# Attention part of a decoder layer: queries scaled once, negated maxima, one reciprocal per head, the normalising multiplications on GpSimd, and one value product in five in full f32 instead of two

## Chip, cores and metric

One core of one Trainium2 chip runs the whole program. The time is the device time of one execution in microseconds (us); of several runs the median counts. Granted TensorE clock 1.00 in a profile is the level of 2.4 GHz, 0.50 that of 1.2 GHz.

## What is computed

One decoder layer over 1024 tokens of width 1024: an input projection, retention heads, sparse-attention heads, an output projection, a gated MLP with a short convolution, an embedding gate and a last norm. The change touches only the sparse-attention heads (8 query heads, 2 key/value groups, head width 64). Cut to what matters, for a block of queries:

```python
s = einsum(qi, ck) * scale                       # compressed keys: 63
p_c = masked_softmax(s, ...);  o_c = einsum(p_c, cv)
s = einsum(qi, ksel) * scale                     # selected keys: with 16 blocks of 64, all of them
p_s = masked_softmax(s, ...);  o_s = einsum(p_s, vsel)
s = einsum(qi, kwi) * scale                      # window of 512 keys
p_w = masked_softmax(s, ...);  o_w = einsum(p_w, vwi)
o = gates[0] * o_c + gates[1] * o_s + gates[2] * o_w

def masked_softmax(s, mask):
    s = where(mask, s, -inf)
    m = max(s);  m = where(isfinite(m), m, 0)
    e = exp(s - m)
    return e / maximum(sum(e), 1e-30)
```

## The kernel before

The kernel is written engine by engine, with semaphores by hand, and each engine runs its instructions in the order written. A product of two f32 values is made of f32r products of a high part and a low part: ScalarE (ACT) copies a tile to its high part, VectorE (DVE) subtracts to get the low part (helper `low`, L1813).

The attention part takes 16 **rounds**, v = 0 to 15: round v is the token tile t = v // 2 (128 queries) and the group v % 2, with four heads. A head has two branches. Branch 0 is the selected keys, (t+1)·128 columns of scores in PSUM banks 0 and 1; branch 1 is the window (up to 640 columns) and the 63 compressed keys, in banks 2 and 3. Heads times branches give 8 **slots** a round, numbered n. For slot n:

- TensorE (PE) makes the scores (`qk`, L1334 to L1347). It may do so when the exponentials of slot n-2, which read the same banks, are done.
- DVE takes the maxima (L1861; L1863 and L1864) and makes the bias of the exponentials `nb` (L1869).
- ACT makes the exponentials (L932; L936 and L939) into `prob` in SBUF, with their sums in `den`.
- DVE, one slot later, guards the sums (L1874), inverts them (L1879) and multiplies `prob` by the inverse and the gate (L1889; L1893 and L1896).

The probabilities of round v are used during round v+1, from its second slot on: PE transposes them 128 keys at a time (`turn_p`, L1261, four heads at once, into one of three PSUM banks), ACT copies the bank (`p_high`, L949), and PE multiplies the values by it (`output`). A list written by `plan_attention` sets the order: turn j, then output j-2, spread over the 8 slots; round v has 3, 5, 7, 9, 11, 12, 13 or 14 tiles of keys for t = 0 to 7. A tile is **whole** or **split**. A whole tile is copied once to `ptw` and multiplied in full f32 (L1377, one instruction that the trace shows as two records). A split tile is copied to its high part `pth`, DVE makes the low part `ptl` (`p_low`, L1813), and PE makes two f32r products (L1379, L1380). `pth` with `ptl` has two places, `ptw` has two more; the copy of a tile waits until the output that used its place before is done (`freed_by`). Within a slot the order is, on PE: turns and outputs, then the scores of the next slot; on ACT: copies, then the exponentials; on DVE: maxima, guard, bias, inverse, low parts, then the multiplications.

```python
def whole(st):
    return st[0] == "turn_p" and st[2] % 5 in (0, 2)
```

Of the kernel before, what the change touches and what calls it, by code (L numbers as in the profile page):

```python
# [15 lines left out]
P = 128  # L16
S = 1024
# [6 lines left out]
G = 2  # L24
RG = QH // G
# [3 lines left out]
WIN_T = 4  # L29
# [79 lines left out]
def build(nc, xt, x, pt, pos, cst_d, wmix_d, wffn_d, gnw, w_in, cpos, ck_w1, ck_w2, cv_w1, cv_w2,  # L109
# [8 lines left out]
    with ctx:  # L118
        def sem(name):
            return ctx.enter_context(nc.semaphore(name))  # L120
# [102 lines left out]
        comb = a.put("comb", [P, 2, 2 * P], F32)  # L223
        mx = a.put("mx", [P, 4, 2], F32)
        nb = a.put("nb", [P, 4, 2], F32)
        den = a.put("den", [P, 4, 2], F32)
        rd = a.put("rd", [P, 4, 2], F32)
        rd2 = a.put("rd2", [P, 4, 2], F32)
        assert a.at <= 229344, a.at


# [158 lines left out]
        def ret_slots(s, k, table):  # L390
# [17 lines left out]
        tr_full, tr_h, tr_l = sem("tr_full"), sem("tr_h"), sem("tr_l")  # L408
        qk_done, nb_done, exp_done, norm_done, pv_done = (
            sem("qk_done"), sem("nb_done"), sem("exp_done"), sem("norm_done"), sem("pv_done"))  # L410
        swap_done, csum_done, nsah_done, nsal_done = sem("swap_done"), sem("csum_done"), sem("nsah_done"), sem("nsal_done")

        h_in, wfb_in = sem("h_in"), sem("wfb_in")
# [57 lines left out]
        def whole(st):  # L471

            return st[0] == "turn_p" and st[2] % 5 in (0, 2)

        outs_of = {(v, j): n for n, (v, j) in enumerate(st[1:] for st in plan if st[0] == "output")}

# [207 lines left out]
        def _(pool):  # L686
# [45 lines left out]
            for s in range(NS + 1):  # L732
                for k in range(NK):
# [3 lines left out]
                        ret_load(0)  # L737
                    ret_slots(s, k, table)

            for t in range(NT):  # L740
# [9 lines left out]
        def _(act):  # L750
# [158 lines left out]
            def q_split_high(st):  # L909
                v = st[1]  # L910
                act.wait_ge(aqr_in[v % 2], 16 * (v // 2 + 1))
                if v:
                    act.wait_ge(tr_full, turns_of["turn_q", v - 1] + 1)
                nc.scalar.activation(aq2[:, :, 0], aqr[:, v % 2].rearrange("p (r d) -> p r d", r=RG), ACT.Copy).then_inc(aqh_done, 1)

            def q_turned(st):
                v = st[1]
# [5 lines left out]
            def exponentials(v, i):  # L923
                n, t = 2 * RG * v + i, v // G
                r_, br = divmod(i, 2)
                act.wait_ge(nb_done, n + 1)
                if v >= 2:
                    act.wait_ge(tr_full, turns_of["turn_p", v - 2, len(key_tiles(v - 2)) - 1] + 1)
                s_, pr = ps[:, 2 * br:2 * br + 2, :].rearrange("p a n -> p (a n)"), prob[:, v % 2, r_]
                m = n % 4  # L930
                if br == 0:
                    nc.scalar.activation(pr[:, 0:(t + 1) * P], s_[:, 0:(t + 1) * P], ACT.Exp, bias=nb[:, m, 0:1],  # L932
                                         scale=SCALE, accum_out=den[:, m, 0:1]).then_inc(exp_done, 1)
                else:
                    w = (t - max(0, t - WIN_T) + 1) * P
                    nc.scalar.activation(pr[:, S:S + w], s_[:, 0:w], ACT.Exp, bias=nb[:, m, 0:1], scale=SCALE,  # L936
                                         accum_out=den[:, m, 0:1])
                    at = S + (WIN_T + 1) * P
                    nc.scalar.activation(pr[:, at:at + NCMP], s_[:, 5 * P:5 * P + NCMP], ACT.Exp, bias=nb[:, m, 1:2],  # L939
                                         scale=SCALE, accum_out=den[:, m, 1:2]).then_inc(exp_done, 1)  # L940

            def p_high(st):
                at = place_of[st]
# [167 lines left out]
        def _(pe):  # L1111
# [237 lines left out]

            def p_turn(st):  # L1350
                v, j = st[1:]
                _, _, at, w = key_tiles(v)[j]
                pe.wait_ge(norm_done, 2 * RG * (v + 1))
                turn_free(st)
                for r_ in range(RG):
                    mm = transpose_f(ps[0:w, turn_bank(st), r_ * P:(r_ + 1) * P], prob[:, v % 2, r_, at:at + w])
                mm.then_inc(tr_full, 1)
# [217 lines left out]
        def _(dve):  # L1575
# [274 lines left out]
            def q_split_low(st):  # L1850
                v = st[1]
                dve.wait_ge(aqh_done, v + 1)
                low(aq2[:, :, 1], aqr[:, v % 2].rearrange("p (r d) -> p r d", r=RG), aq2[:, :, 0]).then_inc(aql_done, 1)

            def row_max(v, i):
                n, t, br = 2 * RG * v + i, v // G, i % 2
                dve.wait_ge(qk_done, n + 1)
                m = n % 4
                s_ = ps[:, 2 * br:2 * br + 2, :].rearrange("p a n -> p (a n)")
                if br == 0:  # L1860
                    return mark(nc.vector.reduce_max(mx[:, m, 0:1], s_[:, 0:(t + 1) * P], AX_X))  # L1861
                w = (t - max(0, t - WIN_T) + 1) * P
                nc.vector.reduce_max(mx[:, m, 0:1], s_[:, 0:w], AX_X)  # L1863
                return mark(nc.vector.reduce_max(mx[:, m, 1:2], s_[:, 5 * P:5 * P + NCMP], AX_X))  # L1864

            def exp_bias(v, i, maxima):
                m, w = (2 * RG * v + i) % 4, 1 + i % 2
                dve.wait_ge(dve_chain, maxima)
                nc.vector.tensor_scalar(nb[:, m, 0:w], mx[:, m, 0:w], FLOOR, -SCALE, ALU.max, ALU.mult).then_inc(nb_done, 1)  # L1869

            def guard_sum(v, i):
                n, w = 2 * RG * v + i, 1 + i % 2
                dve.wait_ge(exp_done, n + 1)
                return mark(nc.vector.tensor_scalar(rd[:, n % 4, 0:w], den[:, n % 4, 0:w], 1e-30, None, ALU.max))  # L1874

            def invert_sum(v, i, guarded):
                m, w = (2 * RG * v + i) % 4, 1 + i % 2
                dve.wait_ge(dve_chain, guarded)
                return mark(nc.vector.reciprocal(rd2[:, m, 0:w], rd[:, m, 0:w]))  # L1879

            def normalize(v, i, inverted):

                n, (t, g_), (r_, br) = 2 * RG * v + i, divmod(v, G), divmod(i, 2)
                m, hd = n % 4, g_ * RG + r_
                dve.wait_ge(dve_chain, inverted)
                pr = prob[:, v % 2, r_]
                if br == 0:
                    p_ = pr[:, 0:(t + 1) * P]
                    nc.vector.tensor_scalar(p_, p_, rd2[:, m, 0:1], gates[:, t, hd, 1:2], ALU.mult, ALU.mult).then_inc(norm_done, 1)  # L1889
                else:  # L1890
                    width = (t - max(0, t - WIN_T) + 1) * P
                    p_ = pr[:, S:S + width]
                    nc.vector.tensor_scalar(p_, p_, rd2[:, m, 0:1], gates[:, t, hd, 2:3], ALU.mult, ALU.mult)  # L1893
                    at = S + (WIN_T + 1) * P
                    p_ = pr[:, at:at + NCMP]
                    nc.vector.tensor_scalar(p_, p_, rd2[:, m, 1:2], gates[:, t, hd, 0:1], ALU.mult, ALU.mult).then_inc(norm_done, 1)  # L1896

            def p_low(st):
                at = place_of[st]
# [32 lines left out]
            q_split_low(("split_q", 0))  # L1932
            for n, slot in enumerate(slots):
                lows = [st for st in slot if st[0] in ("turn_p", "turn_ret") and not whole(st)]
                if n < 2 * RG * NV:
                    maxima = row_max(*divmod(n, 2 * RG))
                if 0 < n <= 2 * RG * NV:
                    guarded = guard_sum(*divmod(n - 1, 2 * RG))
                if n < 2 * RG * NV:
                    exp_bias(*divmod(n, 2 * RG), maxima)  # L1940
                if 0 < n <= 2 * RG * NV:
                    inverted = invert_sum(*divmod(n - 1, 2 * RG), guarded)
                for st in lows:
                    {"turn_p": p_low, "turn_ret": ret_low}[st[0]](st)
                if 0 < n <= 2 * RG * NV:
                    normalize(*divmod(n - 1, 2 * RG), inverted)
# [183 lines left out]
```

## Time and profile before

| | |
|---|---|
| median of 3 runs | 1711.2 us (1708.43 to 1711.42) |
| profiled execution, its time | 1707.47 us |
| its span | 1705.7 us |
| PE busy over the span | 1638.8 us (96%) |
| DVE busy | 1038.6 us (61%) |
| ACT busy | 628.3 us (37%) |
| GpSimd (POOL) busy | 78.1 us (5%) |

The shares are means over parts that differ. The attention rounds lie at about 432 to 747 us of the span. PE's busy time holds the overlap of pipelined matmuls and can hold waits of a few tenths of a microsecond, so the distance from one PE start to the next says more than it.

### The profile page before, as it was taken

The page shows a single profiled execution, that of the slowest core. Times are in us where ns is not written, and L with a number is a line of the kernel's source. Part 1 is how long each engine was busy: PE and PEld are TensorE (multiplying, and loading weights), DVE is VectorE, ACT ScalarE, POOL GpSimd, SP SyncE. Part 2 cuts the span into 40 slices and gives each one's busy share as a digit, 9 for nine tenths or more (in the row PEclk, how much of TensorE's full clock was granted, in tenths as well). Part 3 has the DMA queues.
Part 4 walks back from the last instruction along what each step waited for, and adds up shares of the span by engine and source line. Part 5 has one row for each costly group of instructions (what it writes and reads, how often), then busy time and mean ns, then how long its engine had stood idle before and what let it go on. Part 6 is the DMA issues. An engine that isn't in the chain of part 4 may idle for free.

```text
span 1705.7 us, 22210 instructions
## 1 busy us (share of the span) xinstructions
PE 1638.8 (96%) x8157; PEld 1326.4 (78%) x8157; DVE 1038.6 (61%) x2063; ACT 628.3 (37%) x1173; POOL 78.1 (5%) x126
## 2 busy tenths in 40 slices
PE   8899999998789999999999999999999999999997
PEld 6688888888556776678888888888888888888885
DVE  6833556655799999964345555555556565556432
ACT  6214443344677777752222211221221122114221
POOL 0111221121000000000000000000000000000000
PEclk9899999998799999999999999999999999999998
DMA  5433233225000000060121211111121111122000
GB/s 197 130 99 117 93 109 103 82 92 190 25 23 17 13 13 1 1 235 1 40 72 38 74 37 37 58 52 37 37 74 37 37 46 65 37 72 102 25 38 37
DMA packets 48989, 110.62 MB, mean 65 GB/s; under 512 B 8848, under 2 KB 17040, under 8 KB 48912
## 3 DMA queue, kind: packets, MB, share of 16 engines
q1 hardware_dynamic: 41488, 85.47, 15.0%
q0 software_dynamic: 7424, 24.12, 4.2%
q8 instruction: 48, 0.79, 0.2%
q14 instruction: 29, 0.24, 0.0%
HBM read 89.65 MB, written 19.92 MB: 64 GB/s over the span
## 4 chain that ended last, share of the span: by engine, by line
PE 85%; DVE 6%; ACT 2%; issue 2%; DVEq 0%; POOLq 0%; POOL 0%; ACTq 0%
PE ps L1461 27%; PE ps L1115 14%; PE ps L1117 14%; PE ps L1116 14%; PE ps L1261 4%; PE ps L1377 3%; PE ps L1334 2%; PE ps L1340 1%; PE ps L1448 1%; PE ps L1284 1%; PE ps L1379 1%; PE ps L1120 1%; PE ps L1380 1%; DVE mx L1863 1%; DVE ptl L1813 1%
## 5 line engine op out<-in xcount | busy, mean ns | idle before, releaser
L2003 DVE TENSOR_TENSOR h<-h,ps 128x512 f32<-128x512 f32 x336 | 225.4, 686 | 148.7 <-PE ps L1117 147.5
L1461 PE MATMUL ps<-htl,wuh 128*128 128x512 f32 x672 | 209.7, 393 | 0.0
L1461 PE MATMUL ps<-hth,wuh 128*128 128x512 f32 x672 | 209.6, 393 | 0.0
L1461 PE MATMUL ps<-hth,wul 128*128 128x512 f32 x672 | 209.6, 393 | 0.0
L1115 PE MATMUL ps<-wh,xth 128*128 128x512 f32 (+1 forms) x448 | 186.7, 417 | 14.8 <-DVE wl L1595 13.2
L1117 PE MATMUL ps<-wh,xtl 128*128 128x512 f32 (+1 forms) x448 | 170.8, 381 | 0.0
L1116 PE MATMUL ps<-wl,xth 128*128 128x512 f32 (+1 forms) x448 | 170.3, 380 | 0.0
L1059 ACT ACTIVATE ffh<-ffa 128x1024 fp32r<-128x1024 f32 x22 | 23.3, 1060 | 369.8 <-DVE ffa L2030 369.8
L1461 PEld LDWEIGHTS ps<-hth,wuh 128*128 128x128 f32 x672 | 126.3, 188 | 29.3
L1461 PEld LDWEIGHTS ps<-hth,wul 128*128 128x128 f32 x672 | 126.2, 188 | 29.1
L1461 PEld LDWEIGHTS ps<-htl,wuh 128*128 128x128 f32 x672 | 126.3, 188 | 28.8
L1116 PE MATMUL ps<-wdl,ffh 128*128 128x512 f32 x352 | 139.5, 396 | 0.0
L1117 PE MATMUL ps<-wdh,ffl 128*128 128x512 f32 x352 | 139.1, 395 | 0.0
L1115 PE MATMUL ps<-wdh,ffh 128*128 128x512 f32 x352 | 139.1, 395 | 0.0
L2020 DVE SCALAR_TENSOR_TENSOR act__166<-gate,taps,act__166 128x1024 f32<-128x1024 f32 x22 | 28.3, 1285 | 128.6 <-ACT act__166 L1052 128.6
L1115 PEld LDWEIGHTS ps<-wh,xth 128*128 128x128 f32 x448 | 86.2, 192 | 23.9 <-DVE xtl L1603 7.5
L1261 PE MATMUL ps<-cst,prob 128*128 128x128 f32 (+1 forms) x592 | 88.7, 278 | 9.7 <-DVE retl L1813 7.8
L1117 PEld LDWEIGHTS ps<-wh,xtl 128*128 128x128 f32 x448 | 85.3, 190 | 16.3
L1334 PE MATMUL ps<-aks,aqt 128*128 128x512 f32 (+3 forms) x192 | 80.7, 420 | 16.1 <-ACT prob L939 14.5
L1261 PEld LDWEIGHTS ps<-cst,prob 128*128 128x128 f32 (+1 forms) x592 | 69.4, 142 | 33.8 <-issue 24.5
L1116 PEld LDWEIGHTS ps<-wl,xth 128*128 128x128 f32 x448 | 86.3, 193 | 8.7
L1115 PEld LDWEIGHTS ps<-wdh,ffh 128*128 128x128 f32 x352 | 66.2, 188 | 15.8
(270 smaller groups left out, 3180.2 us busy)
## 6 DMA issues: line engine op xcount, KB each, us to landing
wuraw<-in_w_up SPq DMA_DIRECT2D x44, 512.0 KB, 5.0
wraw<-in_w_in SPq DMA_DIRECT2D x48, 256.0 KB, 3.3
proj_d<-stage POOLq DMA_DIRECT2D x48, 256.0 KB, 2.3
wdraw<-in_w_down SPq DMA_DIRECT2D x22, 512.0 KB, 3.6
rin<-proj_d POOLq DMA_DIRECT2D x32, 256.0 KB, 4.2
xraw<-in_xt SPq DMA_DIRECT2D x16, 256.0 KB, 6.4
owraw<-in_w_out SPq DMA_DIRECT2D x8, 512.0 KB, 5.7
h<-in_x SPq DMA_DIRECT2D x1, 4096.0 KB, 15.9
```

The lines of the kernel that those rows point to most:

```text
L1059: nc.scalar.activation(ffh[:, u], ffa[:], ACT.Copy).then_inc(ffh_done, 1)
L1115: first = nc.tensor.matmul(out, wh_, xh_, start=start, stop=False)
L1116: nc.tensor.matmul(out, wh_, xl_, start=False, stop=False)
L1117: return first, nc.tensor.matmul(out, wl_, xh_, start=False, stop=stop)
L1120: return nc.tensor.transpose(out.bitcast(F32R), in_, ident_r[:])
L1261: return nc.tensor.transpose(out, in_, ident_f[0:n, 0:n])
L1284: mm = nc.tensor.matmul(ps[:, 6 + i, half * G * NCMP:(half + 1) * G * NCMP], cw1[:, i, j, half * P:(half + 1) * P], cb[:, i, j], start=(j ...
L1334: nc.tensor.matmul(ps[:, bank, 0:w], q_, aks[:, br, g_, at:at + w], start=True, stop=False)
L1377: mm = nc.tensor.matmul(out_, vals.bitcast(F32), ptw[0:w, at], start=first, stop=last)
L1461: mm = nc.tensor.matmul(ps[:, 2 * part + half, :], w_, x_[:, k, half * 512:(half + 1) * 512], start=(k == 0 and i == 0), stop=(k == NK - 1 ...
L2003: nc.vector.tensor_tensor(hh, hh, ps[:, 4 + o_ % 4, :], ALU.add).then_inc(dn_add, 1)
L2020: nc.vector.scalar_tensor_tensor(act_[:], gate[:, 1:S + 1], taps[:, u, 1:2], act_[:], ALU.mult, ALU.add).then_inc(conv_mid, 1)
```

## The change

Five edits, all in the attention rounds. The scale goes into the high and low parts of the queries, so the exponentials need none. The maxima come out negated, straight into `nb` for two of the three; the third goes through one small minimum. The sums of a head's three branches are guarded and inverted once, every second slot. The multiplications of `prob` go to GpSimd, which runs three a head, waiting for the inverse; a turn of a branch-0 tile waits for all but the last of them. And a tile is whole only where its number is a multiple of five.

```diff
-        den = a.put("den", [P, 4, 2], F32)
-        rd = a.put("rd", [P, 4, 2], F32)
-        rd2 = a.put("rd2", [P, 4, 2], F32)
+        den = a.put("den", [P, 4, 3], F32)
+        rd = a.put("rd", [P, 4, 3], F32)
...
-            return st[0] == "turn_p" and st[2] % 5 in (0, 2)
+            return st[0] == "turn_p" and st[2] % 5 == 0
...
+            def normalize(v, r_):
+
+                n, (t, g_) = RG * v + r_, divmod(v, G)
+                hd = g_ * RG + r_
+                pool.wait_ge(inv_done, INV0 + n + 1)
+                pr = prob[:, v % 2, r_]
+                p_ = pr[:, 0:(t + 1) * P]
+                nc.gpsimd.tensor_scalar(p_, p_, rd[:, n % 4, 1:2], gates[:, t, hd, 1:2], ALU.mult, ALU.mult).then_inc(norm_done, 1)
+                p_ = pr[:, S:S + (t - max(0, t - WIN_T) + 1) * P]
+                nc.gpsimd.tensor_scalar(p_, p_, rd[:, n % 4, 2:3], gates[:, t, hd, 2:3], ALU.mult, ALU.mult)
+                at = S + (WIN_T + 1) * P
+                p_ = pr[:, at:at + NCMP]
+                nc.gpsimd.tensor_scalar(p_, p_, rd[:, n % 4, 0:1], gates[:, t, hd, 0:1], ALU.mult, ALU.mult).then_inc(norm_done, 1)
...
-                pe.wait_ge(norm_done, 2 * RG * (v + 1))
+                pe.wait_ge(norm_done, 2 * RG * (v + 1) - (br == 0))
...
-                    return mark(nc.vector.reduce_max(mx[:, m, 0:1], s_[:, 0:(t + 1) * P], AX_X))
+                    nc.vector.reduce_max(nb[:, m, 0:1], s_[:, 0:(t + 1) * P], AX_X, negate=True).then_inc(nb_done, 1)
+                    return
                 w = (t - max(0, t - WIN_T) + 1) * P
-                nc.vector.reduce_max(mx[:, m, 0:1], s_[:, 0:w], AX_X)
-                return mark(nc.vector.reduce_max(mx[:, m, 1:2], s_[:, 5 * P:5 * P + NCMP], AX_X))
+                maximum = mark(nc.vector.reduce_max(mx[:, m, 1:2], s_[:, 5 * P:5 * P + NCMP], AX_X, negate=True))
+                nc.vector.reduce_max(nb[:, m, 0:1], s_[:, 0:w], AX_X, negate=True)
+                dve.wait_ge(dve_chain, maximum)
+                nc.vector.tensor_scalar(nb[:, m, 1:2], mx[:, m, 1:2], -FLOOR * SCALE, None, ALU.min).then_inc(nb_done, 1)
...
+                if n >= 4:
+                    dve.wait_ge(norm_done, 2 * (n - 4) + 2)
+                nc.vector.reciprocal(rd[:, n % 4], den[:, n % 4]).then_inc(inv_done, 1)
```

On DVE, two slots of a round of t = 7 stood as follows before: a branch-1 slot and a branch-0 slot of the next head (maxima, guard, bias, inverse, low parts `ptl`, multiplications of `prob`).

```order
L1863 TENSOR_REDUCE mx<-ps 128x1
L1864 TENSOR_REDUCE mx<-ps 128x1
L1874 TENSOR_SCALAR rd<-den 128x1
L1869 TENSOR_SCALAR nb<-mx 128x2
L1879 RECIPROCAL rd_122<-rd 128x1
L1889 TENSOR_SCALAR prob<-prob,rd_122,gates 128x1024
L1861 TENSOR_REDUCE mx<-ps 128x1
```

With the change the same two slots of that round read:

```order
L1885 TENSOR_REDUCE mx<-ps 128x1
L1886 TENSOR_REDUCE nb<-ps 128x1
L1888 TENSOR_SCALAR nb<-mx 128x1
L1882 TENSOR_REDUCE nb<-ps 128x1
L1894 TENSOR_SCALAR den<-den 128x1
L1901 RECIPROCAL rd<-den 128x3
L1832 TENSOR_TENSOR ptl<-ps,pth 128x512 x2
```

The large multiplications are gone from DVE's row, the guard and the inverse stand in every second slot, and there are more low parts.

On PE, a round of t = 7 reads so before, from the output of tile 1 on (L1379, L1380: output of a split tile; L1261: a turn; L1334 to L1342: scores of the next slot; L1377: output of a whole tile, here tile 2; then turn 5 and the output of tile 3).

```order
L1379 MATMUL ps<-pth,av_105 128x512
L1380 MATMUL ps<-ptl,av_105 128x512
L1261 MATMUL ps<-cst,prob 128x128 x4
L1334 MATMUL ps<-aks,aqt 128x512
L1340 MATMUL ps<-akx,aqt 128x512
L1334 MATMUL ps<-aks,aqt 128x512
L1340 MATMUL ps<-akx,aqt 128x512
L1342 MATMUL ps<-masks_b,ident_b 128x128
L1377 MATMUL ps<-ptw,av_105 128x512
L1261 MATMUL ps<-cst,prob 128x128 x4
L1379 MATMUL ps<-pth,av_105 128x512
L1380 MATMUL ps<-ptl,av_105 128x512
```

And so with the change, at the same place.

```order
L1398 MATMUL ps<-pth,av_105 128x512
L1399 MATMUL ps<-ptl,av_105 128x512
L1280 MATMUL ps<-cst,prob 128x128 x4
L1353 MATMUL ps<-aks,aqt 128x512
L1359 MATMUL ps<-akx,aqt 128x512
L1353 MATMUL ps<-aks,aqt 128x512
L1359 MATMUL ps<-akx,aqt 128x512
L1361 MATMUL ps<-masks_b,ident_b 128x128
L1398 MATMUL ps<-pth,av_105 128x512
L1399 MATMUL ps<-ptl,av_105 128x512
L1280 MATMUL ps<-cst,prob 128x128 x4
L1398 MATMUL ps<-pth,av_105 128x512
```

Tile 2 is split now. Tile 4, turned ahead of the scores, is a split tile in both; its place in `pth` was tile 1's before, whose output stands ahead of that turn, and is tile 2's now, whose output stands behind the scores.

## Rows read from the trace of the kernel before

**Rows 1.** The page, busy time by engine: us, share, instructions.

```profile
PE 1638.8 (96%) x8157; PEld 1326.4 (78%) x8157; DVE 1038.6 (61%) x2063; ACT 628.3 (37%) x1173; POOL 78.1 (5%) x126
DVE  6833556655799999964345555555556565556432
```

**Rows 2.** Windows: stretch, its length, busy (instructions) by engine, PE clock, DMA.

```profile
432.67:443.19 10.52, 7.83 (x40) 7.07 (x39) 8.34 (x46) 5.50 (x24) 0.00 (x0) 0.50 0.08 25
443.19:548.39 105.20, 89.75 (x530) 62.74 (x530) 99.62 (x388) 77.89 (x247) 0.00 (x0) 0.96 0.07 20
548.39:703.83 155.44, 150.23 (x918) 109.36 (x917) 146.11 (x413) 118.01 (x287) 0.00 (x0) 1.00 0.03 9
703.83:747.50 43.67, 41.03 (x229) 27.99 (x227) 32.70 (x78) 29.80 (x63) 0.00 (x0) 1.00 0.35 133
```

**Rows 3.** Timeline of DVE: first maxima of rounds 5, 6, 14 and 15.

```profile
497.79 0.55 DVE L1861 TENSOR_REDUCE mx<-ps 128x1 f32<-128x384 f32 x1
513.75 0.68 DVE L1861 TENSOR_REDUCE mx<-ps 128x1 f32<-128x512 f32 x1
679.08 1.22 DVE L1861 TENSOR_REDUCE mx<-ps 128x1 f32<-128x1024 f32 x1
703.83 1.22 DVE L1861 TENSOR_REDUCE mx<-ps 128x1 f32<-128x1024 f32 x1
```

**Rows 4.** Lines by form, 431 to 748 us: busy, mean ns, idle before.

```profile
L1813 DVE TENSOR_TENSOR ptl<-ps,pth 128x512 fp32r<-128x512 f32 x72 | 49.0, 682 | 14.5 <-ACT pth L949 13.8
L949 ACT ACTIVATE pth<-ps 128x512 fp32r<-128x512 f32 x72 | 43.1, 598 | 17.9 <-PE ps L1261 17.2
...
L1893 DVE TENSOR_SCALAR prob<-prob,rd,gates 128x640 f32<-128x640 f32 x32 | 19.5, 608 | 0.4
...
L1869 DVE TENSOR_SCALAR nb<-mx 128x2 f32<-128x2 f32 x64 | 10.8, 169 | 0.0
...
L932 ACT ACTIVATE prob<-ps,nb 128x1024 f32<-128x1024 f32 x8 | 8.9, 1112 | 0.5 <-DVE nb L1869 0.5
...
L1889 DVE TENSOR_SCALAR prob<-prob,rd,gates 128x1024 f32<-128x1024 f32 x8 | 6.4, 806 | 0.1
```

**Rows 5.** Timeline of round 5: one branch-1 slot, from scores to scores.

```profile
502.76 0.43 PE L1334 MATMUL ps<-aks,aqt 128*128 128x384 f32 x1
...
503.47 0.21 PE L1347 MATMUL ps<-masks_b,ident_b 128*128 128x64 bf16 x1
...
504.81 0.55 DVE L1863 TENSOR_REDUCE mx<-ps 128x1 f32<-128x384 f32 x1
...
505.72 0.58 ACT L936 ACTIVATE prob<-ps,nb 128x384 f32<-128x384 f32 x1
...
506.84 0.42 PE L1334 MATMUL ps<-aks,aqt 128*128 128x384 f32 x1
```

**Rows 6.** Timeline of PE, a stretch in which it does not wait.

```profile
727.16 1.02 PE L1377 MATMUL ps<-ptw,av 128*128 128x512 f32 x2
728.02 0.60 PE L1261 MATMUL ps<-cst,prob 128*63 128x128 f32 x4
728.38 0.48 PE L1379 MATMUL ps<-pth,av 128*128 128x512 f32 x1
728.69 0.40 PE L1380 MATMUL ps<-ptl,av 128*128 128x512 f32 x1
728.93 1.02 PE L1377 MATMUL ps<-ptw,av 128*128 128x512 f32 x2
```

**Rows 7.** POOL's arithmetic by line: ns min/median/max, first and last start.

```profile
L722 POOL TENSOR_TENSOR gst<-gst,cst x8: 1663/1665/2032, 176.7 to 393.5; 128x8 f32<-128x8 f32 x8
L742 POOL TENSOR_TENSOR hst<-hst,cst x8: 540/544/571, 777.5 to 842.9; 128x1 f32<-128x1 f32 x8
```

**Rows 8.** Waits, 431 to 748 us: waiter, releaser, total us, times, longest.

```profile
PE ps L1261 <- DVE retl L1813: 7.8, 6, 1.8
...
PEld ps L1261 <- DVE prob L1896: 3.8, 9, 1.6
...
PE ps L1261 <- DVE prob L1896: 1.7, 2, 1.1
```

More of the change, by code:

```diff
@@ L410, in build @@
             sem("qk_done"), sem("nb_done"), sem("exp_done"), sem("norm_done"), sem("pv_done"))
+        inv_done, INV0 = red_done, 2
         swap_done, csum_done, nsah_done, nsal_done = sem("swap_done"), sem("csum_done"), sem("nsah_done"), sem("nsal_done")
@@ L738, in _ @@
                     ret_slots(s, k, table)
+            def normalize(v, r_):
[10 more added lines that the diff above has]
+                nc.gpsimd.tensor_scalar(p_, p_, rd[:, n % 4, 0:1], gates[:, t, hd, 0:1], ALU.mult, ALU.mult).then_inc(norm_done, 1)
+            for v in range(NV):
+                for r_ in range(RG):
+                    normalize(v, r_)
             for t in range(NT):
@@ L913, in q_split_high @@
                     act.wait_ge(tr_full, turns_of["turn_q", v - 1] + 1)
-                nc.scalar.activation(aq2[:, :, 0], aqr[:, v % 2].rearrange("p (r d) -> p r d", r=RG), ACT.Copy).then_inc(aqh_done, 1)
+                nc.scalar.activation(aq2[:, :, 0], aqr[:, v % 2].rearrange("p (r d) -> p r d", r=RG), ACT.Copy,
+                                     scale=SCALE).then_inc(aqh_done, 1)
             def q_turned(st):
@@ L929, in exponentials @@
                 s_, pr = ps[:, 2 * br:2 * br + 2, :].rearrange("p a n -> p (a n)"), prob[:, v % 2, r_]
-                m = n % 4
+                m, q = n % 4, n // 2 % 4
                 if br == 0:
                     nc.scalar.activation(pr[:, 0:(t + 1) * P], s_[:, 0:(t + 1) * P], ACT.Exp, bias=nb[:, m, 0:1],
-                                         scale=SCALE, accum_out=den[:, m, 0:1]).then_inc(exp_done, 1)
+                                         accum_out=den[:, q, 1:2]).then_inc(exp_done, 1)
                 else:
                     w = (t - max(0, t - WIN_T) + 1) * P
-                    nc.scalar.activation(pr[:, S:S + w], s_[:, 0:w], ACT.Exp, bias=nb[:, m, 0:1], scale=SCALE,
-                                         accum_out=den[:, m, 0:1])
+                    nc.scalar.activation(pr[:, S:S + w], s_[:, 0:w], ACT.Exp, bias=nb[:, m, 0:1],
+                                         accum_out=den[:, q, 2:3])
                     at = S + (WIN_T + 1) * P
                     nc.scalar.activation(pr[:, at:at + NCMP], s_[:, 5 * P:5 * P + NCMP], ACT.Exp, bias=nb[:, m, 1:2],
-                                         scale=SCALE, accum_out=den[:, m, 1:2]).then_inc(exp_done, 1)
+                                         accum_out=den[:, q, 0:1]).then_inc(exp_done, 1)
             def p_high(st):
@@ L1351, in p_turn @@
                 v, j = st[1:]
-                _, _, at, w = key_tiles(v)[j]
-                pe.wait_ge(norm_done, 2 * RG * (v + 1))
+                br, _, at, w = key_tiles(v)[j]
+                pe.wait_ge(norm_done, 2 * RG * (v + 1) - (br == 0))
                 turn_free(st)
@@ L1852, in q_split_low @@
                 dve.wait_ge(aqh_done, v + 1)
-                low(aq2[:, :, 1], aqr[:, v % 2].rearrange("p (r d) -> p r d", r=RG), aq2[:, :, 0]).then_inc(aql_done, 1)
+                nc.vector.scalar_tensor_tensor(aq2[:, :, 1], aqr[:, v % 2].rearrange("p (r d) -> p r d", r=RG), SCALE,
+                                               aq2[:, :, 0].bitcast(F32), ALU.mult, ALU.subtract).then_inc(aql_done, 1)
             def row_max(v, i):
@@ L1860, in row_max @@
                 if br == 0:
-                    return mark(nc.vector.reduce_max(mx[:, m, 0:1], s_[:, 0:(t + 1) * P], AX_X))
+                    nc.vector.reduce_max(nb[:, m, 0:1], s_[:, 0:(t + 1) * P], AX_X, negate=True).then_inc(nb_done, 1)
+                    return
                 w = (t - max(0, t - WIN_T) + 1) * P
-                nc.vector.reduce_max(mx[:, m, 0:1], s_[:, 0:w], AX_X)
-                return mark(nc.vector.reduce_max(mx[:, m, 1:2], s_[:, 5 * P:5 * P + NCMP], AX_X))
[L1866 to L1877, printed above, removed]
-                dve.wait_ge(dve_chain, guarded)
[L1879 to L1896, printed above, removed]
@@ new lines, in row_max, with guard_sum @@
+                maximum = mark(nc.vector.reduce_max(mx[:, m, 1:2], s_[:, 5 * P:5 * P + NCMP], AX_X, negate=True))
+                nc.vector.reduce_max(nb[:, m, 0:1], s_[:, 0:w], AX_X, negate=True)
+                dve.wait_ge(dve_chain, maximum)
+                nc.vector.tensor_scalar(nb[:, m, 1:2], mx[:, m, 1:2], -FLOOR * SCALE, None, ALU.min).then_inc(nb_done, 1)
+            def guard_sum(v, r_):
+                n = RG * v + r_
+                dve.wait_ge(exp_done, 2 * n + 2)
+                return mark(nc.vector.tensor_scalar(den[:, n % 4, 0:1], den[:, n % 4, 0:1], 1e-30, None, ALU.max))
@@ L1898, in p_low, with invert_sum @@
+            def invert_sum(v, r_, guarded):
+                n = RG * v + r_
+                dve.wait_ge(dve_chain, guarded)
+                if n >= 4:
+                    dve.wait_ge(norm_done, 2 * (n - 4) + 2)
+                nc.vector.reciprocal(rd[:, n % 4], den[:, n % 4]).then_inc(inv_done, 1)
             def p_low(st):
@@ L1934, in _ @@
                 lows = [st for st in slot if st[0] in ("turn_p", "turn_ret") and not whole(st)]
+                behind = n // 2 - 1
+                due = 0 <= behind < RG * NV
                 if n < 2 * RG * NV:
[L1936 to L1942, printed above, removed]
+                    row_max(*divmod(n, 2 * RG))
+                if n % 2 == 0 and due:
+                    guarded = guard_sum(*divmod(behind, RG))
+                    invert_sum(*divmod(behind, RG), guarded)
                 for st in lows:
                     {"turn_p": p_low, "turn_ret": ret_low}[st[0]](st)
-                if 0 < n <= 2 * RG * NV:
-                    normalize(*divmod(n - 1, 2 * RG), inverted)
                 for st in slot:
```

## The prediction, made blind

> **What bounds the kernel now.** I read the page first, then windows cut at the rounds, then lines by form, and last the timeline. The page shows PE 96% busy over the span and DVE 61%, but DVE's row of slices stands at 9 in the sixth part of the span where the attention rounds lie [rows 1]. The change touches nothing else, so only those 315 us can move. The windows split them in three [rows 2]. In round 0 PE runs at clock 0.50 and nobody is full. In rounds 1 to 7 DVE is busy 99.6 of 105.2 us and PE 89.8: DVE is the bound. In rounds 8 to 14 both are full, PE 150.2 of 155.4 us and DVE 146.1. The last stretch is round 15 and the turns and outputs behind it, PE 41.0 of 43.7.
>
> How DVE holds the others up is seen in one slot of round 5 [rows 5]. The scores of a branch-1 slot start at 502.76 and their last matmul at 503.47 (with its 0.21: 503.68). Their maxima start only at 504.81, the exponentials at 505.72, and the next scores in these banks at 506.84. That loop is 4.08 us a head, and 1.13 us of it (504.81 − 503.68) is the maxima standing behind low parts and multiplications on DVE. Four heads are 16.3 us, and round 5 lasts 513.75 − 497.79 = 16.0 us [rows 3]: the loop is the round.
>
> At t = 7 it is PE's own work. Start to next start, an output of a whole tile costs 728.02 − 727.16 = 0.86 us, a turn 0.36, a split output 728.93 − 728.38 = 0.55 [rows 6]. Round 14 lasts 24.75 us [rows 3].
>
> **The change, part by part.**
>
> *Multiplications off DVE.* 192 instructions leave. Per head at t = 7 they are 0.81 for 1024 columns, 0.61 for 640 and some 0.3 for 63 [rows 4]; with them go half the guards and inverses and most of the bias steps (0.17 each). I count some 6 us a round at t = 0 and 9 at t = 7, about 110 us of DVE's 287. What it is worth is what the loop loses. In rounds 1 to 7 the maxima's 1.13 us of waiting a head falls; I take half of it, 0.55, because low parts stay in front of them: 28 heads, −15.4 us. In rounds 8 to 14 DVE frees no more than PE then leaves idle. PE's idle time there is 5.2 us, and a part of its waits hides in modelled ends; I take −5.
>
> *Fewer whole tiles.* A whole tile leaves wherever its number modulo 5 is 2: 16 in the tiles that rounds 8 to 14 turn, 3 in round 15 and 3 behind it. Each saves PE 0.86 − 0.55 = 0.31 us. PE is the bound there: −5.0 and −1.9. It adds a low part of 0.68 us [rows 4] to DVE for each of 30 tiles, 20 us, hidden under the 110 that went; were DVE still full it would cost all of them.
>
> *Only two places for split tiles.* This is the part that the diff hides. Now four tiles of five need a place of `pth`, and there are still two. The copy of tile 3 waits for the output of tile 1, that of tile 4 for output 2, and so on for 8, 9 and 13: the output that PE does right behind that turn. Where the list puts a slot's end between them, PE makes the next scores first. Then ACT's copy of tile 4 stands until the scores and output 2 are done, and this slot's exponentials stand behind it. From the end of output 2: copy 0.60 [rows 4], exponentials 1.11 [rows 4] and some 0.35 of hand-overs, 2.1 us, against 1.35 us that PE still has to do (two turns of 0.4 and a split output, 0.55). PE or the loop stands about 0.8 us. At t = 2 the exponentials are shorter and so is PE's own work; I take 0.85 throughout. By the list there are 2 such places a round for tails of t = 1 and of t = 7, 2 or 1 for t = 2, 3 and 4, 1 for t = 5, 0 or 2 for t = 6: 19 while exponentials run. 19 × 0.85 = +16 us. Before there were none: tile 4's place was tile 1's.
>
> *GpSimd's price.* No row shows a large multiplication there. Its rows are powers: 0.54 us for one column and 1.67 for eight [rows 7], 0.16 us a column, and that is the upper bound, far off (the 71,616 columns of `prob` would take 11 ms). The lower is DVE's 0.81 us for 1024 columns, under 0.8 ns a column. Between these I take 1.2 ns, the row of one plain DVE pass (1024 columns in 1.22 us [rows 3]), since a streaming multiplication is nearer to that than to a power. Then a head of t = 7 takes GpSimd 2.1 us of its 6, and it is hidden. What counts is the last head of a round, for which the first turn waits: guard 0.14, inverse 0.17, a hand-over and the first multiplication, 1.6 us at t = 7, against 1.4 before (with 0.61 + 0.3 on DVE), and 0.6 against 1.1 at t = 0. Over 16 rounds that is nothing. PE's waits for DVE's last multiplication are 5.5 us in all today [rows 8].
>
> The Trainium skill (GPSIMD Engine Reference, "Performance versus the Vector engine") gives about 1.8 GpSimd cycles an element at 1.2 GHz for a tight loop, 1.5 ns a column, and 2.6 for two inputs, 2.2 ns. By the first the term would be +0.3 us a round, by the second about +1; no run here shows it yet, and my sum does not use it.
>
> *Scale and maxima.* The scale is free on ACT; on DVE one form replaces another of the same size. In a branch-1 slot one small step stays (0.15), in a branch-0 slot none. They are in the 110 us.
>
> **Sum.** −15.4 − 5 − 5.0 − 1.9 + 16 = −11.3 us. The profiled execution took 1707.5 us, so it would take 1696; the median of the runs is 3.7 us above it, and I forecast **1700 us**.
>
> **The rivals.**
>
> *The places cost nothing, the relief is whole.* If ACT has time to spare for the late copies (it is idle a quarter of the time, 77.9 of 105.2 busy [rows 2]), the +16 falls away: −27, 1684 us. Against it: copies are in order ahead of exponentials.
>
> *The places cost more than DVE's relief gives.* DVE's low part of the late tile stands ahead of the next slot's maxima, too, so a second exponential can be late. The relief is 27.3 us over 19 places, so the change loses once a place costs more than 1.44 us. At 2.0 us: +38 − 27, 1722 us. For it: PE is full at t ≥ 4, and any new wait there is paid at once.
>
> *GpSimd becomes the bound.* A round of t = 7 has 6908 columns; at 24.75 us that is 3.6 ns a column. At 4 ns rounds of t ≥ 4 lengthen by 1 to 3 us and the first turn of each waits 2 to 3 us more, in place of the gain: about 1730 us. Against it only that a power is no multiplication.
>
> *DVE and GpSimd stand in each other's way.* If a DVE instruction on SBUF waits for a running GpSimd one, the 64 small steps of the bias, which lie in the loop, can each wait. With GpSimd busy a third of the time and half of a 0.8 us multiplication left, that is 64 × 0.13 = 9 us, and the subtractions `nsal` and of the queries (31) 4 more: 1712 us, no change. The Trainium skill (SBUF — State Buffer, "Who interferes with whom") says of this that DVE instructions in a two-port mode or with two SBUF inputs wait for GpSimd, and reductions and those reading PSUM do not; by it the queries' and `nsal`'s 31 surely wait, the one-column steps perhaps.
>
> **Numbers.** Forecast, gain of 5 to 24 us: 0.45, its own range 1687 to 1706. Full relief, 24 us or more: 0.20. Dear places: 0.15. GpSimd the bound: 0.07. In each other's way, or gains and losses even: 0.13. A measurement of this kernel tells 0.2% (3.4 us) from no change. Faster 0.66 (the first two), same 0.12, slower 0.22. For eight in ten the range goes from inside full relief, 1679, to between the even case and the dear places at 2 us, 1718.
>
> **What would show it.** DVE's busy time in the stage near 190 us instead of 287, with GpSimd at 70 to 110. Maxima in a slot like that of [rows 5] starting within 0.6 us of their scores. ACT waiting for PE's outputs (L1398, L1399 of the new file) ahead of copies to `pth`, some 20 times with about 1 us each: without these rows the places cost nothing. PE waiting for GpSimd at the first turn of a round 0 to 1 us. A split output should still take PE 0.55 us from start to next start. Multiplications of 1024 columns near 1.2 us; over 3 the forecast is wrong, as it is if the maxima start as late as today behind the extra low parts. The parts outside the rounds should keep their length within 1 us.

## The result: 0.45% slower, and the profile after

The changed kernel takes 1719.2 us, the median of 6 runs (1716.5 to 1719.9); the kernel before, run beside it, takes 1711.2. The ratio is 1.0045, with an interval of 1.0032 to 1.0058. Forecast were 1700 us and faster. Executions of one kernel fall on levels that go with the mean granted clock (the changed kernel took 1716.5 us at 0.985 and 1719.0 to 1719.9 at 0.980 and 0.981), so differences are given between medians and, where it matters, at like clock. The page of the changed kernel, busy time by engine, and its rows of slices for DVE and the clock:

```profile
PE 1636.6 (95%) x8157; PEld 1331.9 (78%) x8157; DVE 971.2 (57%) x1709; ACT 624.7 (36%) x1173; POOL 203.4 (12%) x318
DVE  6733555655567677764355555655555555556432
PEclk9999999998689999999999999999999999999999
```

Windows of the changed kernel, cut at the same round starts as [rows 2] (stretch, length, PE, PEld, DVE, ACT, POOL busy, clock, DMA):

```profile
432.39:442.12 9.73, 7.84 (x40) 7.08 (x39) 4.33 (x24) 5.15 (x23) 3.80 (x9) 0.50 0.07 21
442.12:554.41 112.29, 94.74 (x530) 70.02 (x530) 71.68 (x227) 76.84 (x246) 45.73 (x84) 0.87 0.06 19
554.41:713.82 159.41, 145.98 (x915) 108.72 (x916) 114.44 (x262) 116.13 (x288) 63.62 (x84) 1.00 0.03 9
713.82:759.20 45.38, 39.70 (x230) 28.06 (x228) 29.40 (x58) 29.51 (x65) 12.20 (x15) 1.00 0.33 128
```

DVE is freed (99.6 to 71.7 us and 146.1 to 114.4; over all rounds 287 to 220, where near 190 was forecast), PE has no more to do, and yet rounds 1 to 7 take 112.3 us instead of 105.2 and rounds 8 to 14 take 159.4 instead of 155.4. No engine is full: something waits. The waits of the changed kernel, 431 to 765 us, name it (waiter, releaser, total us, times, longest):

```profile
DVE ptl L1832 <- ACT pth L968: 58.7, 72, 2.1
ACT pth L968 <- PE ps L1399: 52.4, 44, 2.4
...
PE ps L1353 <- ACT prob L958: 15.2, 20, 1.7
...
PE ps L1353 <- ACT prob L951: 12.2, 12, 1.8
```

ACT's copy to `pth` (L968) waits for an output (L1399) for 52.4 us in all, 44 times. By the list, 48 copies want a place whose output stands behind their own turn, and for 20 of them (18 while exponentials run) the next scores stand in between; before, there was no such copy, and the copies waited for turns alone [rows 4]. One of these waits, in round 4, from the timeline of the changed kernel:

```profile
491.60 0.41 PE L1353 MATMUL ps<-aks,aqt 128*128 128x384 f32 x1
...
492.30 0.20 PE L1366 MATMUL ps<-masks_b,ident_b 128*128 128x64 bf16 x1
...
492.34 0.48 PE L1398 MATMUL ps<-pth,av 128*128 128x512 f32 x1
...
492.66 0.39 PE L1399 MATMUL ps<-ptl,av 128*128 128x512 f32 x1
...
493.14 0.60 ACT L968 ACTIVATE pth<-ps 128x512 fp32r<-128x512 f32 x1 [1.68 <-PE ps L1399]
...
493.64 0.59 ACT L940 ACTIVATE aqt<-ps 128x512 fp32r<-128x512 f32 x1
493.77 0.69 DVE L1832 TENSOR_TENSOR ptl<-ps,pth 128x512 fp32r<-128x512 f32 x1 [1.92 <-ACT pth L968]
494.11 0.58 ACT L951 ACTIVATE prob<-ps,nb 128x384 f32<-128x384 f32 x1
...
494.51 0.55 DVE L1886 TENSOR_REDUCE nb<-ps 128x1 f32<-128x384 f32 x1
...
494.93 0.41 PE L1353 MATMUL ps<-aks,aqt 128*128 128x384 f32 x1 [1.45 <-ACT prob L951]
```

The copy is that of tile 3 and could have gone at 491.5. It waits until PE has made the scores and output 1, since both places of `pth` are taken. Behind it in ACT's order stand the queries' copy and the exponentials of 494.11, and behind the low part on DVE stand the next maxima. PE comes to its next scores only at 494.93, 3.33 us after the last ones, and stands 1.45 us of that.

### The profile page after: what moved, and what is told of

Read it like the earlier page. It is cut to its first block, busy times and chain, and to the rows that moved or that the text cites. A ratio compares the mean times of both kernels' runs of the same rounds, so it can differ in the third digit from the quotient of the medians.

```text
span 1717.0 us, 22108 instructions
## 1 busy us (share of the span) xinstructions
PE 1636.6 (95%) x8157; PEld 1331.9 (78%) x8157; DVE 971.2 (57%) x1709; ACT 624.7 (36%) x1173; POOL 203.4 (12%) x318
## 3 DMA queue, kind: packets, MB, share of 16 engines
q1 hardware_dynamic: 41488, 85.47, 14.9%
## 4 chain that ended last, share of the span: by engine, by line
PE 87%; ACT 3%; DVE 3%; issue 2%; POOL 0%; DVEq 0%; ACTq 0%; POOLq 0%
PE ps L1480 27%; PE ps L1134 14%; PE ps L1136 13%; PE ps L1135 13%; PE ps L1280 4%; PE ps L1353 2%; PE ps L1396 2%; PE ps L1359 2%; PE ps L1398 2%; PE ps L1399 1%; PE ps L1467 1%; PE ps L1303 1%; PE ps L1139 1%; PE ps L1361 1%; ACT prob L955 1%
## 5 line engine op out<-in xcount | busy, mean ns | idle before, releaser
L1078 ACT ACTIVATE ffh<-ffa 128x1024 fp32r<-128x1024 f32 x22 | 23.3, 1060 | 369.8 <-DVE ffa L2032 369.8
L1832 DVE TENSOR_TENSOR ptl<-ps,pth 128x512 fp32r<-128x512 f32 (+1 forms) x112 | 76.1, 686 | 59.9 <-ACT pth L968 58.7
L764 POOL TENSOR_TENSOR fst<-fst,cst 128x1 f32<-128x1 f32 x8 | 4.4, 550 | 849.7 <-DVE fst L2060 849.7
```

## The experiments

After the result I held two theories. **A**: the places. Once four tiles of five are split and there are two places, the copy waits for an output that stands behind the scores, and that costs about twice what I took for it. **B**, the rival: the loss lies in what the change added for good, the multiplications on GpSimd (their speed, or their standing in DVE's way) or the extra low parts. All ratios are against the kernel before, run on the same chip.

**Three places in `pth`, one in `ptw`** (same SBUF in all):

```diff
-        NPT = 2
+        NPT = 3
-        NPW = 2
+        NPW = 1
```

> The changed kernel with three places for split tiles (pth, ptl) and one for whole tiles, nothing else. Theory A, that the two places make ACT's copies and so the exponentials wait for outputs that stand behind the next scores: the 52 us of ACT waiting for the second product of an output (L1399) fall under 10 us, and the time falls from 1719 by 20 to 30 us to 1690 to 1700. Rival B, that the added low parts, the GpSimd multiplications or the new form of the maxima cost the time whatever the places: the waits may move, the time stays within 5 us of 1719. Rival C, GpSimd's multiplications late at the start of a round: 1719 less at most 5 us, since PE waits for them 5 us in all.

1688.2 us, ratio 0.9876 [0.986, 0.9893]: 31.0 us less than the changed kernel, from two numbers (26 to 29 at like clock: 1687.9 against 1716.5 at the higher, 1693.9 against 1719.5 at the lower). Waits of this kernel, 431 to 765 us, and its timeline at the same place of round 4:

```profile
ACT pth L968 <- PE ps L1280: 31.3, 65, 1.3
DVE ptl L1832 <- ACT pth L968: 25.2, 52, 1.5
```

```profile
484.94 0.59 ACT L968 ACTIVATE pth<-ps 128x512 fp32r<-128x512 f32 x1
...
485.19 0.41 PE L1353 MATMUL ps<-aks,aqt 128*128 128x384 f32 x1
...
485.90 0.60 ACT L951 ACTIVATE prob<-ps,nb 128x384 f32<-128x384 f32 x1
485.94 0.48 PE L1398 MATMUL ps<-pth,av 128*128 128x512 f32 x1
...
486.31 0.55 DVE L1886 TENSOR_REDUCE nb<-ps 128x1 f32<-128x384 f32 x1
...
486.83 0.42 PE L1353 MATMUL ps<-aks,aqt 128*128 128x384 f32 x1
```

The copy does not wait, the exponentials start 0.71 us behind the scores instead of 2.51, and the next scores come after 1.64 us instead of 3.33. The copy's wait for L1399 is no longer among the rows.

**Two of five tiles whole**, the rest of the change kept, two places each (`st[2] % 5 in (0, 2)`).

> The changed kernel with two whole tiles in five as before and two places each. Theory A: no copy waits for a late output; the relief of DVE is there without the price of the places, but PE does 30 whole tiles more, 0.31 us each: 1692 to 1700. Rival B: the GpSimd multiplications or the maxima are what costs, so the time stays at or above that of before, 1711 to 1720.

1698.9 us, 0.9928 [0.9914, 0.9941]. This is the relief of DVE without any place: 11.8 us under the kernel before by medians, 8.2 between the profiled executions (1707.5 and 1699.2), which are at like clock (0.96 over rounds 1 to 7 in both); most other executions of the kernel before are nearer 1711 and at a lower clock. Its rounds 1 to 7 last 539.34 − 442.46 = 96.9 us and its rounds 8 to 14 154.5, so 8.3 us come from the first and 0.9 from the second.

**One of five whole alone**, in the kernel before (`st[2] % 5 == 0`).

> The kernel before with only its list of whole tiles changed to one in five. Theory A: the places cost here what they cost in the change, and 30 low parts of 0.68 us come on a DVE that is full: 20 to 35 us slower than before, 1731 to 1746. Rival B: only the low parts count, and PE gains 9 us: 1711 to 1725. If this edit is harmless, 1705 to 1711, the change's loss comes from another edit.

1739.4 us, 1.0169 [1.0155, 1.0183]. The part alone is worse than the whole change, and its waits show the same row (L1380 is the output before):

```profile
ACT pth L949 <- PE ps L1380: 44.2, 36, 2.6
```

It mixes two things, the places and 20 us of low parts on a DVE that is full. The last experiment parts them.

**Output j−2 ahead of turn j**, in the changed kernel: the order gives the place back before the copy wants it.

```diff
-                    if j < n:
-                        tail.append(("turn_p", v, j))
                     if j >= 2:
                         tail.append(("output", v, j - 2))
+                    if j < n:
+                        tail.append(("turn_p", v, j))
```

> The changed kernel with each output j-2 put ahead of turn j in the list instead of behind it, two places as in the change. Theory A: the output that frees a place is always ahead of the turn whose copy needs it, so no copy stands behind the next scores; the waits of ACT for L1399 fall under half. Against it the low part of tile j-2 has one turn less of time before its product, which can cost PE some 0.3 us in places: 1697 to 1710. Rival B: no change within 5 us of 1719, or slower.

1705.6 us, 0.9974 [0.9963, 0.9984]: 13.6 us come back, not 31. Waits of this kernel:

```profile
PEld ps L1398 <- DVE ptl L1832: 17.2, 23, 1.8
...
PEld ps L1396 <- ACT ptw L968: 10.6, 12, 1.9
```

The copy no longer waits for the output; now the output waits for its low part or copy, which has one turn less of time. The next run shows whether that is all.

**Both: three places and the output first.**

> The changed kernel with three places for split tiles, one for whole tiles, and each output j-2 ahead of turn j. With three places no copy waits for a late output, so by theory A the order has nothing more to give and can only take from the low parts' lead: 1686 to 1694, not under e1's 1688 by more than 3 us. If the order helps in itself: 1678 to 1684.

1705.7 us, 0.9971 [0.9959, 0.9983], and I had expected 1686 to 1694. With this order a third place is worth nothing, and the order itself costs 17.5 us against 1688.2. So it removes the places' cost and brings another, and it was no clean test of A.

**The multiplications back on DVE**, three for each head in a row, with two of five tiles whole; the other edits stay.

```diff
-                pool.wait_ge(inv_done, INV0 + n + 1)
+                dve.wait_ge(inv_done, INV0 + n + 1)
...
-                nc.gpsimd.tensor_scalar(p_, p_, rd[:, n % 4, 1:2], gates[:, t, hd, 1:2], ALU.mult, ALU.mult).then_inc(norm_done, 1)
+                nc.vector.tensor_scalar(p_, p_, rd[:, n % 4, 1:2], gates[:, t, hd, 1:2], ALU.mult, ALU.mult).then_inc(norm_done, 1)
```

> The e2 kernel (two whole tiles in five, two places each) with the multiplications of prob back on DVE, three a head behind the head's inverse; the other edits stay. It splits the 12 us that e2 gained. Theory A, DVE's relief is what gains and the multiplications (90 us) are nearly all of it: 1707 to 1716. Rival: the small edits (negated maxima, one guard and inverse a head, 20 us of DVE time) give half or more of it: 1700 to 1706. A head's multiplications come in one piece here, so up to 4 us slower than before is possible.

1713.2 us, 1.0017 [1.0008, 1.0026]. Against 1698.9 the place of the multiplications, GpSimd or DVE, is worth 14.3 us, so B's part on GpSimd falls. With the multiplications on DVE the other edits bring no gain, but here a head's three multiplications also stand in one piece, so what scale, maxima and one inverse a head are worth by themselves is not shown.

**No tile whole, three places** (`return False`).

> The changed kernel with three places and every tile split, so no full f32 value product at all: 36 tiles fewer whole, 0.31 us of PE each, 11 us, and 36 low parts of 0.68 us more on DVE, 24 us on top of 220 of 300. Theory A, PE bounds the rounds of t of 4 and more and DVE has room: 7 to 12 us under e1, 1676 to 1681. Rival B, DVE's low parts are again what the outputs and maxima wait for: no faster than e1, 1686 to 1695.

1685.9 us, 0.9849 [0.9834, 0.9864], the best of all, and I had expected 1676 to 1681. Against three places with one tile of five whole it is 2.3 us less by medians and 5 to 7 at like clock (1682.4 and 1682.8 against 1687.9; 1685.9 to 1687.4 against 1693.9). With three places a split tile is still the cheaper one, by less than PE's 0.31 us for each of 36 tiles; what takes the rest was not looked for.

**GpSimd's work made heavier**, with three places: each multiplication is preceded by one of the same columns by 1.0.

```diff
+                nc.gpsimd.tensor_scalar(p_, p_, 1.0, None, ALU.mult).then_inc(twice, 1)
+                pool.wait_ge(twice, 3 * n + 1)
                 nc.gpsimd.tensor_scalar(p_, p_, rd[:, n % 4, 1:2], gates[:, t, hd, 1:2], ALU.mult, ALU.mult).then_inc(norm_done, 1)
```

> The e1 kernel with each of GpSimd's 192 multiplications preceded by one of the same size by 1.0, with a wait between the two, so GpSimd has some 250 us of work instead of 125. If GpSimd is hidden but for the first turn of a round, each round's first turn waits for one more multiplication (0.4 us at t = 0, 1.2 us at t = 7) and the hand-over: 10 to 20 us over e1, 1698 to 1708, and in the rounds of small t GpSimd (12 a round doubled, some 6 us times 2) nearly fills the round. If GpSimd's time were free altogether: 1688 to 1691. If it already bounded the rounds: over 1750.

1797.5 us, 1.0513 [1.0499, 1.0527], and I had expected at most 1708. The page, then POOL's lines by form and the first turn's wait (431 to 800 us):

```profile
PE 1653.7 (92%) x8157; PEld 1350.9 (75%) x8157; DVE 974.5 (54%) x1709; ACT 629.2 (35%) x1173; POOL 421.2 (23%) x510
```

```profile
L754 POOL TENSOR_SCALAR prob<-prob,rd,gates 128x640 f32<-128x640 f32 x32 | 28.2, 882 | 3.2
...
L748 POOL TENSOR_SCALAR prob<-prob 128x1024 f32<-128x1024 f32 x8 | 22.2, 2770 | 5.3 <-DVE rd L1908 5.3
```

```profile
PEld ps L1287 <- POOL prob L750: 85.1, 14, 9.3
PE ps L1287 <- POOL prob L750: 82.6, 14, 9.1
```

It was no doubling. The multiplication by 1.0 takes 2770 ns for 1024 columns where the real one takes 1196, so GpSimd's 125 us (203.4 − 78.1) became 343 (421.2 − 78.1), more than the 296 that the rounds last with three places (431.9 to 728.1), and it was the bound. So the rival of the prediction in which GpSimd is the bound comes about with nearly three times today's load; from what load on it does was not tried.

**Output in the same slot as its turn**: two places, as in the change, but where turn j is of number 3 or 4 modulo 5, output j−2 is put into turn j's slot, so no scores stand between them.

```diff
+                put = {}
                 for x, st in enumerate(tail):
-                    slots[base + per * x // len(tail)].append(st)
+                    put[st] = base + per * x // len(tail)
+                    if st[0] == "output" and (st[2] + 2) % 5 in (3, 4) and ("turn_p", v, st[2] + 2) in put:
+                        put[st] = put["turn_p", v, st[2] + 2]
+                    slots[put[st]].append(st)
```

> The changed kernel with two places, and only this moved: where the copy of tile j (j modulo 5 is 3 or 4) waits for output j-2 and the list had put that output into the next slot, the output is put into the slot of turn j, so that it stands ahead of the scores. Theory A in its narrow form (only the 19 places where scores come between cost much): most of the 31 us between the change and e1 come back, 1690 to 1700. Rival A2, that two places are too few everywhere, for each split tile in a row: less than half comes back, 1704 to 1716.

1698.3 us, 0.9932 [0.9917, 0.9948]. Waits of this kernel, with L1403 the output:

```profile
ACT pth L972 <- PE ps L1403: 33.7, 43, 1.6
```

The copy still waits for an output 43 times, but for 33.7 us instead of 52.4, and 20.9 of the 31 us come back (at like clock 23.0 of 28.6, 1716.5 to 1693.5, or 20.5 of 25.6). By the list the 48 copies still want a place from an output behind their turn, but no scores stand between any more. So it is not the waiting for an output that costs most, but the scores between turn and output. The rest, 5 to 6 us at like clock against three places, was not taken apart.

**The pair once more**, one profile each of the changed kernel and of the one with three places, to part the places from the clock.

> The changed kernel once more, a look at TensorE's granted clock. In its first trace the clock falls to 0.50 within 456 to 480 us and 496 to 508 us, which e1's does not. If this belongs to the kernel (PE idle at these places), it falls again at the same places and the time is 1716 to 1720. If it is chance, rounds 2 and 5 come out up to 3 us shorter each.

> The e1 kernel once more, for the same question: clock 1.00 from 456 us on as in its first trace and 1687 to 1689, or a fall to 0.50 in round 2 and some 3 to 6 us more.

1720.6 and 1693.0 us. In the second one the clock falls in round 2 as it does in the changed kernel, so the two can be laid side by side. Rounds 1 and 2 together differ by 0.1 us. Rounds 3 to 14, in which 16 places with scores in between lie by the list, are together 23.3 us longer in the change. That is 1.46 us a place. Round 15 and the turns and outputs behind it hold four more and are 3.4 us longer. Round by round, from the first maxima:

| places with scores between | rounds: us longer in the change |
|---|---|
| none | 13: 0.0 |
| one | 3: 2.0; 6: 1.7; 7: 1.7; 10: 1.2; 11: 1.2; 12: 1.2 |
| two | 4: 3.6; 5: 3.3; 8: 3.0; 9: 1.8; 14: 2.5 |

Round 13 is the control. By the list four of its copies want a place from an output that stands directly behind their own turn, and three are seen waiting, up to 1.3 us, but no scores stand between, and the round is as long as with three places. Its start and end in the change, then with three places:

```profile
666.02 1.07 DVE L1882 TENSOR_REDUCE nb<-ps 128x1 f32<-128x896 f32 x1
...
689.79 1.21 DVE L1882 TENSOR_REDUCE nb<-ps 128x1 f32<-128x1024 f32 x1
```

```profile
644.40 1.07 DVE L1882 TENSOR_REDUCE nb<-ps 128x1 f32<-128x896 f32 x1
...
668.17 1.21 DVE L1882 TENSOR_REDUCE nb<-ps 128x1 f32<-128x1024 f32 x1
```

**One of five whole and three places, in the kernel before**: it fills the last field of a square of four.

> The kernel before with one value product in five whole (as in the experiment that did that alone, 1739.4 us), and with three score places and one other, so no second place. Theory A (the two places are the loss: 1.36 us a place and the clock's falls, 31 us in the pair of the change with and without): the part's loss is mostly places here too, so 1708 to 1716 us, and the wait of the pth copy for L1380 is gone from the chain of waits. Rival (the low parts, some 20 us more VectorE work in a kernel whose VectorE is already what the end waits for, are the loss alone): 1730 us or more. In between, the two parts divide it, and the difference to 1739.4 is what the places cost beside a full VectorE.

1711.8 us, 1.0011 [1.0002, 1.002]. With it:

| us | two places | three places | the places cost |
|---|---|---|---|
| without the other edits | 1739.4 | 1711.8 | 27.7 |
| with them | 1719.2 | 1688.2 | 31.0 |

The places cost nearly the same beside a full DVE and beside a free one (27.6 us at like clock in the second row, 1720.6 against 1693.0). Splitting more tiles costs nothing there but places (1711.8 against 1710.9), where the low parts eat what PE wins; beside a free DVE it wins 10.7 us (1698.9 to 1688.2). B's part on low parts falls too, and A stands.

## Why the prediction was wrong

The mechanism and its sign were named; the sizes were not right. The terms:

| term | forecast | by medians | at like clock | by |
|---|---|---|---|---|
| DVE's relief | −20.4 | −11.8 | −8.2 | two of five whole against before |
| of it rounds 1 to 7 | −15.4 | | −8.3 | the same, round starts |
| of it rounds 8 to 14 | −5 | | −0.9 | the same |
| fewer whole tiles | −6.9 | −10.7 | −11.3 | three places against two of five whole |
| the places | +16 | +31.0 | +27.6 | the change against three places |

**The step that failed** is "19 × 0.85 = +16 us" for the places, and in it the price. The list has 18 such places while exponentials run, not 19 (round 3 has one, not two), and two behind them. A place cost 1.46 us in rounds 3 to 14 and (23.3 + 3.4) / 20 = 1.34 over all 20, not 0.85. The places together cost 27.6 us at like clock, 11.6 more than forecast. The other terms were forecast at −27.3 and measured at −19.5 there, which costs another 7.8; by medians it is 15 and 4.8. With the places at +16 the change would have been 3 to 7 us faster, so it is their price that turned the sign. The rival of dear places is what came about. It said that the change loses once a place costs more than 1.44 us; with the smaller relief it loses from 19.5 / 20 = 0.98 us on. (The prediction's own chances for its first two cases add up to 0.65, where it says 0.66.)

Why 0.85 was too little is in the row of 491.60 above. I set 2.1 us of ACT's work behind the output against 1.35 us that PE still had. In that slot PE had one turn left, not two turns and an output; between the copy and the exponentials stood the queries' copy of 0.59 us, which I had not counted; and the maxima at 494.51 were late behind the low part, so the next exponentials were, too. The prediction names the last of these under the rival, and gave it 0.15. How the price divides among the three was not measured.

**The relief** was also too large. DVE's busy time fell by 67 us, not by about 97. The rows that left are 121 us by their own durations and the 30 new low parts 20, but neighbouring rows overlap by some 0.1 us, and I had set durations against busy time. The maxima do start at once now, as forecast: 486.18 in the kernel with three places, 0.08 us after their scores. But that slot does not lose the whole of it. The bias is ready at 486.91, and ACT's next exponentials start at 487.61, behind a copy that waits 0.53 us for its turn. Over all rounds the exponentials' waits for the bias fell from 28.7 us (19.1 + 9.6) to 14.9 (12.1 + 2.8), while the copies' waits for turns stayed at 37.5 us in both kernels (20.3 + 17.2 before, 31.3 + 6.2 with three places). What the loop waits for in place of DVE is not shown by these sums, and no run took that wait away.

**GpSimd** was right: 1196 ns for 1024 columns against 1.2 ns a column. POOL's lines by form in the changed kernel:

```profile
L749 POOL TENSOR_SCALAR prob<-prob,rd,gates 128x640 f32<-128x640 f32 x32 | 28.0, 875 | 0.0
L752 POOL TENSOR_SCALAR prob<-prob,rd,gates 128x63 f32<-128x63 f32 x64 | 27.6, 431 | 0.0
L747 POOL TENSOR_SCALAR prob<-prob,rd,gates 128x1024 f32<-128x1024 f32 x8 | 9.6, 1196 | 32.1 <-DVE rd L1901 32.1
```

A head of t = 7 takes 2.5 us of its 6. The two figures worked out from the Trainium skill (GPSIMD Engine Reference, "Performance versus the Vector engine"), 1.5 and 2.2 ns a column, do not hold for this form over its lengths: 1.5 fits at 512 columns (768 ns) and is too high at 1024, since the rows grow by 0.84 ns a column from a start of some 0.34 us; 2.2 is too high at both. GpSimd's work is 125 us, where 70 to 110 were forecast. PE's waits for GpSimd at a first turn are 2.8 + 1.8 us in all.

**In each other's way** is real and small. The low part of the queries (L1872, two inputs in SBUF) meets GpSimd in the changed kernel's timeline, first with GpSimd idle, then with it running:

```profile
443.11 0.42 DVE L1872 SCALAR_TENSOR_TENSOR aq<-aqr,aq 128x256 fp32r<-128x256 f32 x1
...
470.44 0.55 POOL L749 TENSOR_SCALAR prob<-prob,rd,gates 128x256 f32<-128x256 f32 x1
470.60 0.67 DVE L1872 SCALAR_TENSOR_TENSOR aq<-aqr,aq 128x256 fp32r<-128x256 f32 x1
470.98 0.57 POOL L752 TENSOR_SCALAR prob<-prob,rd,gates 128x63 f32<-128x63 f32 x1
```

Beside GpSimd it takes 0.67 us instead of 0.42, and the 63 columns of GpSimd that start within it 0.57 us, against 0.41 where nothing runs beside them (at 493.24). The mean over the 15 of them is 493 ns, and with the multiplications on DVE it is 425: 15 × 0.068 = 1.0 us in all. The Trainium skill (SBUF — State Buffer, "Who interferes with whom") has two-input DVE instructions wait for GpSimd's reads, and these rows agree. The one-column steps, which my rival priced at 9 us, do not wait: 143 ns (L1888) here, where 30 of the 64 run beside a multiplication of GpSimd's, and 144 with the multiplications on DVE. The low parts `nsal` never met GpSimd and kept their time (416 ns and 415).

## What to carry to other kernels

When an edit moves items from one kind of buffer to another, count the buffers of each kind and ask, item by item, which operation gives the place back and what stands ahead of it in its engine's order; a place that is returned behind the next stage's work costs that stage's whole hand-over, and here moving one buffer from `ptw` to `pth` turned 0.45% slower into 1.2% faster. Price such a stall by writing out every instruction behind the late one on each engine, not only the one that is wanted. And where a bound is lifted, read what stands next in the loop before counting the whole of it as gain.

## What the runs showed of the hardware

**The clock.** Windows of the changed kernel, and then of the one with three places:

```profile
454.00:462.00 8.00, 5.50 (x41) 4.45 (x41) 6.08 (x21) 7.14 (x26) 3.17 (x8) 0.93 0.06 17
462.00:470.00 8.00, 8.00 (x29) 5.69 (x29) 2.75 (x13) 3.71 (x16) 2.89 (x7) 0.50 0.00 0
...
490.00:496.00 6.00, 4.43 (x29) 3.00 (x27) 2.69 (x9) 2.61 (x8) 2.71 (x5) 1.00 0.00 0
496.00:502.00 6.00, 4.32 (x15) 2.82 (x15) 2.93 (x10) 3.26 (x12) 2.09 (x4) 0.70 0.00 0
```

```profile
454.00:462.00 8.00, 5.52 (x43) 4.47 (x43) 6.46 (x23) 6.72 (x24) 3.42 (x8) 1.00 0.06 17
462.00:470.00 8.00, 6.29 (x43) 4.54 (x41) 5.68 (x23) 6.60 (x24) 3.75 (x8) 1.00 0.14 36
...
490.00:496.00 6.00, 5.08 (x35) 3.54 (x33) 4.95 (x17) 5.52 (x18) 2.87 (x5) 1.00 0.21 60
496.00:502.00 6.00, 6.00 (x41) 4.59 (x41) 4.76 (x14) 4.59 (x14) 3.38 (x6) 1.00 0.03 10
```

The granted clock falls to 0.50 (1.2 GHz) in round 2, and is 0.70 over 496 to 502 us, behind 12 us (484 to 496) in which PE was busy 8.9 us; with three places it was busy 10.3 us there and kept 2.4 GHz. The second fall is in both traces of the changed kernel and in neither of the one with three places; with one of five whole alone, which has the same places, the clock is 0.52 over 502 to 508 us. So the fall goes with the stalls at the places; what it adds to them was not measured by itself. The first fall is something else: behind 5.5 to 5.6 of 8 us it came in one trace of the three-place kernel and not in the other, and round 2 took 14.57 and 11.23 us. That 3.3 us is most of the 5.1 between the two executions (1693.0 and 1687.9); 1.2 more came ahead of the rounds.

**GpSimd's form.** In place and of the same shape, a multiplication by two values from SBUF takes 0.84 ns a column ((1196 − 875) / 384), and one by an immediate 1.0 takes 2.5 ns ((2770 − 1815) / 384, from 1815 ns for 640 columns). Which difference between the two does it, the immediate or the number of operations, no run here tells.
